# One tile of 256 tokens moved from the end of the program to second place

## What is computed

```python
h = rmsnorm(x, g_pre_mix)
z, q, k, v, glow, og = jnp.split(h @ w_in, SPLIT_IDX, axis=-1)
...
mix = jnp.concatenate([pool_out.astype(x.dtype), gla_out.astype(x.dtype)], axis=-1) @ w_o
x = x + rmsnorm(mix, g_post_mix)
f, conv_new = conv_ffn(rmsnorm(x, g_pre_ffn), conv_buf, w_up, w_conv, b_conv, w_down)
x = x + rmsnorm(f, g_post_ffn)
x = x + (p.astype(x.dtype) @ w_ple) * jax.nn.sigmoid(x @ w_ple_gate)
```

## Time and profile before

| | before |
|---|---|
| median of 3 runs | 2514.07 us (2513.3 to 2518.11) |
| profiled execution, its own time | 2515.29 us |
| its span | 2513.5 us |
| PE busy | 2492.4 us (99%) |
| DVE busy | 1542.4 us (61%) |
| ACT busy | 1256.4 us (50%) |
| DMA, share of q1 | 54.2%, 434.82 MB |
| granted clock of PE | 0.999 |

### The profile page before, as it was taken

How to read it: one execution, slowest core, us unless ns; L and a number is a source line. 1 busy time by engine, 2 the same in 40 slices (tenths; PEclk the granted TensorE clock), 3 DMA queues, 4 the chain that set the end, 5 groups by cost and what they waited for, 6 DMA issues and landing times.

```text
span 2513.5 us, 40470 instructions
## 1 busy us (share of the span) xinstructions
PE 2492.4 (99%) x16216; PEld 2429.2 (97%) x16216; DVE 1542.4 (61%) x2479; ACT 1256.4 (50%) x1959; POOL 178.5 (7%) x508
## 2 busy tenths in 40 slices
PE   9999999999999999999999999999999999999999
PEld 8889999989999999999999999999999999999999
DVE  7668765556665554666545466654546664647865
ACT  5455554554444455544445544444545444546554
POOL 4201000100000010000001000000100000010000
PEclk9999999999999999999999999999999999999999
DMA  8555556554444656444465644446564444676665
GB/s 252 181 187 160 183 147 224 195 200 147 151 122 129 217 178 209 151 152 126 125 221 175 214 151 151 123 126 212 177 217 151 144 125 128 206 251 208 192 184 170
DMA packets 128250, 437.40 MB, mean 174 GB/s; under 512 B 13760, under 2 KB 23360, under 8 KB 127552
## 3 DMA queue, kind: packets, MB, share of 16 engines
q1 hardware_dynamic: 128064, 434.82, 54.2%
HBM read 403.48 MB, written 31.28 MB: 173 GB/s over the span
## 4 chain that ended last, share of the span: by engine, by line
PE 95%; DVE 2%; DMA 1%; ACT 1%; issue 0%; POOL 0%; SPq 0%; DVEq 0%; POOLq 0%; ACTq 0%
PE G L1682 29%; PE G L1683 28%; PE G L1684 28%; PE X L1728 2%; PE G L1966 1%; PE G L1967 1%; PE G L1968 1%; PE X L1786 1%; PE X L1678 1%; DMA kept_lo<-w_lo 1%; DVE w_lo L1164 0%; DMA stage<-in_w_up_units_dram 0%; PE X L1792 0%; PE X L1707 0%; PE X L1771 0%
## 5 line engine op out<-in xcount | busy, mean ns | idle before, releaser
L1682 PE MATMUL G<-h_hi,w_hi 128*128 128x384 f32 (+2 forms) x3072 | 997.9, 325 | 6.5 <-DVE w_lo L1164 3.3
L1683 PE MATMUL G<-h_hi,w_lo 128*128 128x384 f32 (+2 forms) x3072 | 988.0, 322 | 0.0
L1684 PE MATMUL G<-h_lo,w_hi 128*128 128x384 f32 (+2 forms) x3072 | 988.0, 322 | 0.0
L749 ACT ACTIVATE w_hi<-stage 128x1024 fp32r<-128x1024 f32 (+1 forms) x457 | 473.2, 1036 | 421.8 <-DMA stage<-in_w_up_units_dram 248.3
L1164 DVE TENSOR_TENSOR w_lo<-stage,w_hi 128x1024 fp32r<-128x1024 f32 (+1 forms) x457 | 546.0, 1195 | 138.8 <-ACT w_hi L749 137.9
L1682 PEld LDWEIGHTS G<-h_hi,w_hi 128*128 128x128 f32 x3072 | 579.6, 189 | 14.0 <-DVE w_lo L1164 4.3
L1683 PEld LDWEIGHTS G<-h_hi,w_lo 128*128 128x128 f32 x3072 | 579.6, 189 | 1.5
L1684 PEld LDWEIGHTS G<-h_lo,w_hi 128*128 128x128 f32 x3072 | 579.5, 189 | 0.0
L1682 PE MATMUL G<-y_hi,w_hi 128*128 128x384 f32 (+2 forms) x1056 | 342.6, 324 | 0.0
L1684 PE MATMUL G<-y_lo,w_hi 128*128 128x384 f32 (+2 forms) x1056 | 339.4, 321 | 0.0
L1683 PE MATMUL G<-y_hi,w_lo 128*128 128x384 f32 (+2 forms) x1056 | 339.3, 321 | 0.0
(11 more groups left out here) (220 smaller groups left out, 2703.9 us busy)
## 6 DMA issues: line engine op xcount, KB each, us to landing
stage<-in_w_up_units_dram SPq DMA_DIRECT2D x264, 512.0 KB, 3.6
w_lo<-kept_lo SPq DMA_DIRECT2D x145, 512.0 KB, 4.8
stage<-in_w_down_units_dram SPq DMA_DIRECT2D x96, 448.0 KB, 3.3
w_whole<-in_w_in_units_dram SPq DMA_DIRECT2D x72, 512.0 KB, 3.9
stage<-in_w_down_units_dram SPq DMA_DIRECT2D x48, 512.0 KB, 3.5
w_hi<-kept_hi SPq DMA_DIRECT2D x40, 512.0 KB, 3.6
w_whole<-in_w_gate_units_dram SPq DMA_DIRECT2D x33, 512.0 KB, 3.8
kept_lo<-w_lo SPq DMA_DIRECT2D x32, 512.0 KB, 5.1
```

The costliest lines, as they stand in the source:

```text
L749: act.activation(w_hi[s][:, 0:parts, :], whole[:, 0:parts, :], ACT.Copy).then_inc(hi_made, 1)
L1682: pe.matmul(ps[:, 0:w], l_hi, r_hi[:, 0:w], start=start, stop=False)
L1683: pe.matmul(ps[:, 0:w], l_lo, r_hi[:, 0:w], start=False, stop=False)
L1684: return pe.matmul(ps[:, 0:w], l_hi, r_lo[:, 0:w], start=False, stop=stop)
```

## The change

The narrow tile of 256 comes second, and tiles 2 to 5 have 384. The constant `NARROW` names it. The lows of odd in units are made again there, and no longer in the last tile, and gate units 3 to 7 of the last tile load their kept lows as all others do. `NATIVE` stays with the last tile. Since one line is added, an instruction of line N before is at line N + 1 afterwards.

```diff
--- before.py
+++ after.py
@@ -29,9 +29,10 @@
 LEVELS = (64, 32, 16, 8, 4, 2, 1)
 
 
-TILES = ((0, 256, NS), (256, 384, 0), (640, 384, 0), (1024, 384, 0), (1408, 384, 0), (1792, 256, 0))
+TILES = ((0, 256, NS), (256, 256, 0), (512, 384, 0), (896, 384, 0), (1280, 384, 0), (1664, 384, 0))
 NT = len(TILES)
 LAST = NT - 1
+NARROW = 1
 TM = 384
 CM = TM // P
 ZM = 16 + 256 + 24 * NSEQ
@@ -120,7 +121,7 @@
 def made_again(unit):
 
     t, kind, m = unit
-    return t == LAST and (kind == "in" and m % 2 == 1 or kind == "gate" and m >= 3)
+    return t == NARROW and kind == "in" and m % 2 == 1
 
 
 UNITS, OUTS, TICKS = plan()
```

## The result

| | before | after |
|---|---|---|
| median of 7 runs each | 2514.95 us | 2522.70 us (2521.82 to 2526.92) |
| profiled execution, its own time | 2515.29 us | 2523.04 us |
| its span | 2513.5 us | 2521.3 us |
| PE busy | 2492.4 us | 2495.7 us |
| DMA | 434.82 MB on q1 | 437.44 MB on q1 |

The ratio is 1.0031, with a 95% interval from 1.0022 to 1.0040. One run of before, of 11,287 us, lies far outside all others; without it the median of before is 2514.51 us. The time grew by 7.8 us, in the median and in the span alike (8.2 in the median if that run is left out); the forecast was 4.9.

What follows compares the result with a forecast made beforehand. The prediction took a full PE with a few holes as the bound; its terms, -3.3 + 5.4 + 1.2 + 0.6 + 0 + 0.9 - 0.5 + 0.6 = +4.9, gave 2519.0 us, range 2513.5 to 2524.

Steps and rivals of the forecast that it cites:

- the DMA rival: Tile 1's o units: DMA becomes the bound, weights land up to 4 us late, 2519.0 + 3.5 = 2522.5; chance 0.12.
- tile 1's four waits: Before tile 1's first up unit: PE's waits for DVE's low halves fall from 5.16 to 1.9 us, -3.3.
- tile 2's wait for up unit 0: Tile 1's narrower gates end sooner, DVE's wide norm chain does not shrink with them; PE waits, +5.4, bounds 4.9 and 6.0.
- tile 2's spread: Spreading the heads' root in tile 2: slack of 0.96 us becomes a wait for ACT, +1.2, bounds 0.3 and 2.
- down stage of tile 1: Now narrow while DVE and ACT prepare a 384-wide tile 2; PE's matmuls are 1.8 us shorter, +0.6, bounds 0 and 2.
- its up stage: Tile 1's up units: narrower y store against tile 2's x load, one against the other, 0, bounds -0.5 and +1.5.
- native gates: Last tile's two native gate units become 384 wide, the products they stand in for 256 wide, +0.9.
- last gates' wait: Last tile's gates 3 to 7 load their lows, so the wait of 0.47 us goes, -0.5.
- behind the last matmul: A sigmoid, two DVE operations and a store at the end, each 384 wide now, +0.6.

Runs made afterwards that it cites:

- The run with the order alone: Changed kernel; on DVE, the low half of tile 2's up unit 0 goes ahead of norm steps 7 and 8 and unit 5's gate operations: 2519.56 us, ratio 1.0020.
- the last run: Changed kernel with the better DVE order at tile 2, x of tile 2 in quarters and tile 1's lows one norm step earlier: 2518.30 us, ratio 1.0010.
- the kernel before with the order alone: Kernel before; in tile 1, DVE makes the low halves of gate units 5 to 7 and up unit 0 earlier: 2513.75 us, ratio 0.9992.
- the same with GpSimd: Kernel before; tile 1's lows of gate units 5 to 7 and up unit 0 earlier, additions for y on GpSimd except last tile: 2514.01 us, ratio 0.9990.

## Why the prediction was right

Right: slower, by DVE's chain at tile 2; 2522.7 is inside the wide range of 2513.5 to 2524 and 3.7 us over the point. It is outside the 2516.5 to 2521.5 that the forecast itself had at 0.60, and stands by chance on the 2522.5 of the DMA rival, whose mechanism is not what made it. By its own terms:

| term | predicted | measured |
|---|---|---|
| tile 1's four waits | -3.3 | -3.18 (5.16 to 1.38 + 0.60) |
| tile 2's wait for up unit 0 | +5.4 | +5.92 |
| tile 2's spread | +1.2 | +0.98 |
| down stage of tile 1 | +0.6 | +0.46 |
| its up stage | 0 | +0.49 (1.00 against 0.51) |
| native gates | +0.9 | +0.65 |
| last gates' wait | -0.5 | -0.47 |
| behind the last matmul | +0.6 | +0.36 |
| sum | +4.9 | +5.2 |
| low clock behind the wait | none | +2.05 |
| o units of tile 1 | none | +1.44, in this execution |
| tile 0 | none | -1.17, in this execution |

**The largest miss is a missing term, not one of the sum.** "PE waits 5.4 us" was priced at 5.4, as if PE went on at full speed behind it. It went on at half, for 2.05 us more. The profile before had no wait over 2.52 us behind tile 0 to learn this from, and the forecast did not ask what a PE that stands still for so long does next. The runs bear the link out in both directions: with PE kept at work the clock stays up, with the narrow tile third it falls in tile 3.

**Tile 2's wait.** PE's part got 7.47 us shorter where 7.7 was forecast, DVE's first norm started 0.58 sooner (0.6 forecast), but the chain from there to the low half got only 0.69 shorter, from 21.18 to 20.49. The forecast let 0.6 of 1.1 us of idleness go "since ACT's high halves also come sooner". They did not help: DVE was idle for 0.30 and 0.90, waiting for them.

```profile
853.04 0.62 DVE L1407 SCALAR_TENSOR_TENSOR h_lo<-xr,const,h_hi 128x384 fp32r<-128x384 f32 x1 [0.30 <-ACT h_hi L916]
...
857.80 0.62 DVE L1407 SCALAR_TENSOR_TENSOR h_lo<-xr,const,h_hi 128x384 fp32r<-128x384 f32 x1 [0.90 <-ACT h_hi L916]
```

With the idleness of before kept, the forecast's own arithmetic gives 6.0, its upper bound. The run with the order alone refines the reading: 3.1 of the 5.92 us stood there because the half came behind norm steps that up unit 0 needs only further on; 2.8 us of waiting stay with either order.

**The rival of the DMA bound** is not shown. Tile 1's o units took 24.47 us in the changed kernel's profile where they took 23.03 in place 5, at a DMA share of 0.85 and 323 GB/s, with one wait of 0.74 for a kept low half and smaller holes. But with the same code for that stage they ran without a wait in 23.03 us at 0.91 and 340 GB/s in the run with another order in tile 2 (469.40 to 492.43), and in 23.03 and 23.04 in the two with matmuls of ones. So a late load costs up to 1.4 us there in some executions and nothing in others; the 3.5 us of the rival did not come. The forecast also argued that the x load and the y store offset each other; the x load costs more, by 0.5 us here.

**Tile 0** differs by -1.17 without any change there. The low clock in it lasted 6.8 us before and 3.4 after, and between 3.4 and 13.7 in the other runs, so spans of single executions can't be compared more finely than that. With it and what is left (-0.1 to +0.2 in several stages) the terms make up the 7.8.

**The native gates and what stands behind the last matmul** were each over-priced by a quarter of a microsecond, with the right sign.

## What to carry to other kernels

When PE's work gets narrower beside a chain of another engine that stays wide, the cover of that chain shrinks by the whole difference; look at what the chain's end waits behind in its own order, since here one operation moved ahead of two norm steps and a gate's operations took 3 of the 6 us back. Price a long wait of PE with what its clock does behind it, and keep it short or filled. A saving in one place (tile 1) and its price in the next (tile 2) both have to be read from the queue in order, and a chain at no slack then takes in every late load. And before a sum of waits is called better or worse, look at the clock behind each: a slower PE hides waits.

## What the runs showed of the hardware

- The granted clock fell to 0.50 with every wait of PE of 4.30 us or more behind tile 0: 5.92, 5.30, 6.32, 6.25 and 4.30 us, one in each of five profiles. It did not fall around waits of 1.85 us or less. Between them it went both ways: it fell at the start of work behind a wait of 2.30 us (the last run) and 0.7 us behind one of 2.70 (the kernel before with the order alone), and not around 2.69 (the same with GpSimd), 2.52 (before) and 2.52 (the narrow tile third). Each time it fell, matmuls ran at half rate for 3 to 5 us behind the wait. In all these cases PE had run at the full clock before the wait; why some of the middle ones brought the low clock and others did not stays open.
- A matmul of ones, 128 columns in float32, takes 0.22 us, more than one of 384 columns in the high and low formats, 0.173.
- The low clock in tile 0 lasted 3.4, 6.8, 10.2 or 13.7 us in all from one profile to the next, and tile 0's down stage began anywhere from 312.1 to 316.1 us, with the same code up to there in all twelve.
- An addition of two SBUF operands of 384 columns on DVE took 0.98 us when it met one on GpSimd, both times in that stretch, and 0.56 otherwise.
- A load of 512 KB took 7.2 us from issue to landing behind one of 1536 KB, and 4.2 as the median of the ten around it.
